# A hybrid decoder trunk on one core: attention's v by token rows for four heads at once, a gate's products in v's places, three low parts of a turn on GpSimd

## What is computed

```python
proj = jnp.einsum('bld,de->ble', x, w_in[l]) + b_in[l]
q_sb, k_sb, v_sb, u_ssm, q_mem, gate_logits = jnp.split(proj, splits, axis=-1)
sb = _stick_breaking_attention(q_sb, k_sb, v_sb)       # 8 heads of 128
p_sb = jnp.einsum('ble,ed->bld', sb, sb_w_out[l])
g = jax.nn.gelu(_s5(u_ssm, ...))
glu_a, glu_b = jnp.split(jnp.einsum('ble,ef->blf', g, ssm_w_glu[l]), 2, axis=-1)
p_ssm = jnp.einsum('ble,ed->bld', glu_a * jax.nn.sigmoid(glu_b), ssm_w_out[l])
p_mem = jnp.einsum('ble,ed->bld', _memory_attention(q_mem, mem, w_kv), mem_w_out[l])
gates = jax.nn.sigmoid(gate_logits).reshape(bsz, seq, 3, D_MODEL)
merged = gates[:, :, 0] * p_sb + gates[:, :, 1] * p_ssm + gates[:, :, 2] * p_mem
```

## Time and profile before

| | us |
|---|---|
| median of 3 runs | 2956.91 (2956.4 to 2957.02) |
| the profiled execution, its own time | 2957.04 |
| its span, first to last instruction | 2955.3 |
| PE busy in the span | 2935.8 |
| DVE busy | 1932.0 |
| ACT busy | 1371.5 |
| POOL busy | 46.6 |

### The profile page before, as it was taken

One profiled execution on the slowest core, in us unless ns is written; L12 is line 12 of the kernel. 1 busy time (PEld: TensorE's weight loads), 2 busy tenths in 40 slices (PEclk: granted clock), 3 DMA queues, 4 the chain that ended last, 5 costly groups with the idle time before them and its releaser, 6 DMA issues.

```text
span 2955.3 us, 37621 instructions
## 1 busy us (share of the span) xinstructions
PE 2935.8 (99%) x14068; PEld 2449.7 (83%) x14068; DVE 1932.0 (65%) x2754; ACT 1371.5 (46%) x1646; POOL 46.6 (2%) x117
## 2 busy tenths in 40 slices
PE   8999999999999999999999999999999999999999
PEld 7888888888888888888888888888888888888887
DVE  8899755555755555555699996555666555555556
ACT  6656544444544444444466554444444444444443
POOL 5000000000000000000000000000000000000000
PEclk9999999999999999999999999999999999999999
DMA  9666565656655555555556565665656555555554
GB/s 252 194 189 179 198 205 194 207 190 212 229 191 192 187 196 185 194 189 190 191 140 170 161 188 195 203 202 198 223 172 213 185 194 189 188 195 185 189 194 142
DMA packets 390020, 568.31 MB, mean 192 GB/s; under 512 B 20408, under 2 KB 194592, under 8 KB 389024
## 3 DMA queue, kind: packets, MB, share of 16 engines
q1 hardware_dynamic: 385712, 554.77, 58.5%
q10 hardware_dynamic: 4208, 12.21, 1.1%
HBM read 558.81 MB, written 8.13 MB: 192 GB/s over the span
## 4 chain that ended last, share of the span: by engine, by line
PE 97%; DVE 1%; ACT 1%; DMA 0%; issue 0%; SPq 0%; ACTq 0%; DVEq 0%
PE banks L1854 26%; PE banks L1856 26%; PE banks L1855 26%; PE banks L1829 9%; PE banks L1832 4%; PE banks L1844 1%; PE banks L2275 1%; PE banks L2209 1%; PE banks L2297 0%; DMA raw<-in_w_in 0%; DVE lo L1206 0%; PE banks L1846 0%; PE banks L2028 0%; PE banks L2040 0%; PE banks L2210 0%
## 5 line engine op out<-in xcount | busy, mean ns | idle before, releaser
L1206 DVE TENSOR_TENSOR lo<-raw,hi 128x1024 fp32r<-128x1024 f32 x1014 | 1232.0, 1225 | 957.5 <-ACT hi L736 870.6
L736 ACT ACTIVATE hi<-raw 128x1024 fp32r<-128x1024 f32 x932 | 977.8, 1059 | 1163.1 <-PE banks L1856 1155.1
L1854 PE MATMUL banks<-hi,xs 128*128 128x512 f32 x2176 | 852.0, 392 | 2.4 <-DVE xs L1349 2.4
L1856 PE MATMUL banks<-hi,xs 128*128 128x512 f32 x2176 | 847.3, 389 | 0.0
L1855 PE MATMUL banks<-lo,xs 128*128 128x512 f32 x2176 | 846.9, 389 | 0.0
L1854 PEld LDWEIGHTS banks<-hi,xs 128*128 128x128 f32 x2176 | 408.5, 188 | 86.6 <-DVE xs L1349 2.9
L1856 PEld LDWEIGHTS banks<-hi,xs 128*128 128x128 f32 x2176 | 408.4, 188 | 85.2
L1855 PEld LDWEIGHTS banks<-lo,xs 128*128 128x128 f32 x2176 | 408.7, 188 | 82.9
L1829 PE MATMUL banks<-xs,hi 128*128 128x512 f32 x960 | 307.1, 401 | 0.5 <-DVE lo L1206 0.5
L1854 PE MATMUL banks<-hi,hT 128*128 128x512 f32 x704 | 274.1, 389 | 0.0
L1856 PE MATMUL banks<-hi,hT 128*128 128x512 f32 x704 | 273.9, 389 | 0.0
(11 more groups left out here) (254 smaller groups left out, 2430.5 us busy)
## 6 DMA issues: line engine op xcount, KB each, us to landing
raw<-in_ffn_w_gate_up SPq DMA_DIRECT2D x176, 1024.0 KB, 5.0
raw<-in_w_in SPq DMA_DIRECT2D x156, 1024.0 KB, 5.2
raw<-in_ffn_w_down SPq DMA_DIRECT2D x88, 1024.0 KB, 4.9
raw<-in_w_o SPq DMA_DIRECT2D x32, 1024.0 KB, 5.0
raw<-in_sb_w_out SPq DMA_DIRECT2D x16, 1024.0 KB, 5.0
raw<-in_mem_w_kv SPq DMA_DIRECT2D x12, 1024.0 KB, 5.8
raw<-in_ssm_w_out SPq DMA_DIRECT2D x8, 1024.0 KB, 5.1
raw<-in_mem_w_out SPq DMA_DIRECT2D x8, 1024.0 KB, 5.1
```

Of the source, the lines that this page charges most:

```text
L736: act.activation(hi[:, hl_slot(ph, c, h), :], raw[:, slot, h * HALF:(h + 1) * HALF], ACT.Copy).then_inc(hi_ready, 1)
L1206: dve.tensor_tensor(lo[:, s, :], raw[:, slot, h * HALF:(h + 1) * HALF], hi[:, s, :].bitcast(F32), ALU.subtract).then_inc(lo_ready, 1)
L1854: pe.matmul(dst, xh, hi[:, s, w], start=first, stop=False)
L1856: return pe.matmul(dst, xl, hi[:, s, w], start=False, stop=last)
```

## The change

- v of heads 0 to 3 is computed in `group_half` form as four new chunks at the end of U, in banks 2 and 3; v of heads 4 to 7 in the old v places c = 2 and 5 of turns 0 and 1 (`wide`). DVE adds the bias and writes four heads at once (`v_rows`). The places c = 2 and 5 of turns 2 and 3 take gate 0. Transposes and copies of v go.
- The BL turn's own filler becomes gate 1 (`second_gate`, banks 0 and 1), and gate 1 leaves its place between the projections 0 and 1 in GLU. The number of chunks of a layer stays: U 8 (was 4), GLU 14 (was 18).
- Banks move: the state inputs to 5, 4, 6, 7; GLU's products to 4, 5, 6, 7, used twice (`GLU_BANK`).
- In BR turns other than the first of layer 0 the second half of chunks 3, 6 and 8 gets its low part from GpSimd (`POOL_AT`), five turns in all; DVE waits for it before it splits the next chunk.

```diff
-    "U": (1, [0, 1, 2, 3], [2] * 4),
+    "U": (1, [0, 1, 2, 3] * 2, [2] * 4 + [1] * 4),
-    "GLU": (1, ([2, 3, 0, 1] * 5)[:18], [1] * 4 + [4] * 2 + [1] * 12),
+    "GLU": (1, ([2, 3, 0, 1] * 4)[:14], [1] * 4 + [4] * 2 + [1] * 8),
-GLU_BANK = (0, 1, 4, 5, 6, 7, 0, 1)
+GLU_BANK = (4, 5, 6, 7, 4, 5, 6, 7)
+WIDE_AT = (2, 5)
+POOL_AT = (2, 5, 7)
...
+                for turn in range(1 - l, 3):
+                    for c in POOL_AT:
+                        gh = chunk_no("BR", l, turn, c + 1) * 2 + 1
+                        pool.wait_ge(hi_ready, gh + 1)
+                        pool.wait_ge(lo_ready, gh + HALF_CREDIT)
+                        pool.tensor_tensor(lo[:, hl_slot("BR", c + 1, 1), :],
+                                           raw[:, PHASES["BR"][1][c + 1], HALF:2 * HALF],
+                                           hi[:, hl_slot("BR", c + 1, 1), :].bitcast(F32), ALU.subtract
+                                           ).then_inc(lo_ready, 1)
...
+                        if shared and c - 1 in POOL_AT:
+                            dve.wait_ge(lo_ready, chunk_no(ph, l, i, c + 1) * 2 + HALF_CREDIT)
+                        if shared and c in POOL_AT:
+                            lo_half(PHASES[ph][1][c + 1], hl_slot(ph, c + 1, 0), 0, chunk_no(ph, l, i, c + 1) * 2)
+                        else:
+                            split_next(ph, l, i, c)
...
+                    def v_rows(g, dst, ready):
+                        dve.wait_ge(half_done, ready)
+                        dve.wait_ge(v_bias_in, 16 * (2 * l + g + 1))
+                        dve.tensor_tensor(dst[:].rearrange("p h m d -> p m h d"),
+                                          banks[:, 2:4, :].rearrange("p m (h d) -> p m h d", d=P),
+                                          v_bias[:].rearrange("p a (h d) -> p a h d", d=P)
+                                          .broadcast_to([P, TT, 4, P]), ALU.add).then_inc(v_ready, 1)
...
+                    pe.wait_ge(bu_copied, n * 4 + 3)
                     for t in range(TT):
                         ins = pe.matmul(S[:, t * T:(t + 1) * T], qm_f[:, t * P:(t + 1) * P], km_f[:], start=True,
                                         stop=True)
                     ins.then_inc(s_done, 1)
                     gemm(1, xs)
-                    gemm(2, xs)
+                    wide(2)
...
-                    got(2)
-                    v_turn(0, v_f, VO)
                     tri(0)
...
                         else:
-                            pe.wait_ge(tile_out, tile_no("GLU", l, 0, 1) + 1 + TILE_CREDIT)
+                            pe.wait_ge(tile_out, tile_no("GLU", l, 0, 2 * t - 3) + 1 + TILE_CREDIT)
...
                 branch_products("GLU", 0, GLU_SPANS, 0)
                 pe.wait_ge(tile_out, tile_no("GLU", l, 0, 7) + 1 + TILE_CREDIT)
-                gate_products("GLU", 0, GLU_SPANS, 1)
                 pe.wait_ge(merge_step, 20 * l + 1)
                 pe.wait_ge(glu_lo, 4 * l + 4)
                 branch_products("GLU", 0, GLU_SPANS, 1)
```

More of the change, by code:

```diff
@@ L454, in branch_turn @@
                                  (w, (t + (3 * SBW // P + 1)) * P), (w, (t + ((3 * SBW + SSMW) // P + 1)) * P)]
[L455 to L458, removed]
+                    for c, at in enumerate(cols):
+                        if at is None:
+                            load_block(ph, i, c, w, 4 * (2 * (t % 2) + WIDE_AT.index(c)),
+                                       2 * SBW + GROUP if t < 2 else GATE_COLS)
+                        else:
+                            load(ph, l, i, c, columns(*at))
+                    if t == 0:
+                        sp.wait_ge(v_ready, 2 * l + 1)
+                        load_v_bias(1)
                 if l == 0:
@@ L501, in _ @@
                 load_branch("GLU", 0, GLU_SPANS, 0, 0)
[L502 to L506, removed]
+                sp.wait_ge(attn_done, 12 * l + 15)
+                load_bias(0, 1)
                 load_branch("GLU", 0, GLU_SPANS, 0, 1)
-                sp.wait_ge(gate_in, 12 * l + 1)
-                load_bias(0, 2)
                 for c in range(4):
                     load_gate_block("GLU", 0, GLU_SPANS, 0, 2, c)
+                    if c == 2:
+                        sp.wait_ge(gate_in, 12 * l + 1)
+                        load_bias(0, 2)
                 load_branch("GLU", 0, GLU_SPANS, 0, 2)
@@ L907, in table @@
                     if q == 0:
[L908 removed]
+                        act.activation(tab[:].rearrange("p a c -> p (a c)"), bank[6][:, :], ACT.Copy).then_inc(tab_out, 1)
                         return
@@ L926, in tile @@
                             bias = bias_col(l, bias_tile)
-                        first_half(ph, l, i, c, bank[c % 2], done(ph, l, i, c), bias, scale)
-                        if l == 0 and turn == 1 and c % 2 and c < 8:
-                            save_mem(c // 2)
+                        k = TILE_AT[c]
+                        first_half(ph, l, i, k, bank[k % 2], done(ph, l, i, c), bias, scale)
+                        if l == 0 and turn == 1 and k % 2:
+                            save_mem(k // 2)
                     def copy_bu(j):
@@ L1027, in branch_turn @@
                     out_hi(0, VO, sbT[:, bass.ds(turn * 2, 1), 0:T])
-                    copy_v(1, S, vm_s, 2)
-                    tile(5, turn * 2 + 17)
+                    copy_vm()
                     softplus(1)
@@ L1103, in _ @@
                     glu_high(t)
-                for c in range(7, 18):
+                for c in range(7, 14):
                     split_next("GLU", l, 0, c)
-                    if c == 12:
+                    if c == 8:
                         gate_tanh(1, 4 * l)
-                    if c == 17:
+                    if c == 13:
                         gate_tanh(2, 4 * l)
@@ L1533, in branch_turn @@
                     split(0)
+                    if turn == 0:
+                        v_rows(0, v_first, chunk_no(ph, l, i, 0) * 2 + HALF_CREDIT)
                     if first:
@@ L1583, in branch_turn @@
                         split(6)
+                        if turn == 1:
+                            v_rows(1, v_last, chunk_no(ph, l, i, 6) * 2 + HALF_CREDIT)
                         scan_states(1, 5, 7)
@@ L1980, in _ @@
                     norm(l - 1, 1, first_state)
+                for c in range(4):
+                    for h in range(2):
+                        k = 4 * c + 2 * h
+                        group_half("U", l, 0, 4 + c, h, xs, k, 2, k == 0, k == KD - 2)
                 def table(q):
@@ L2006, in half, with wide @@
                     def half(c, x_t, h):
+                        k = TILE_AT[c]
                         if h == 0 and (turn or c):
-                            pe.wait_ge(tile_out, tile_no(ph, l, i, c) + 1)
-                        product(ph, l, i, c, h, bank[c % 2], x_t, 8 * h, h == 0, h == 1)
+                            pe.wait_ge(tile_out, tile_no(ph, l, i, k) + 1)
+                        product(ph, l, i, c, h, bank[k % 2], x_t, 8 * h, h == 0, h == 1)
+                    def wide(c):
+                        at = 2 * (turn % 2) + WIDE_AT.index(c)
+                        if at == 0:
+                            pe.wait_ge(v_ready, 2 * l + 1 + turn // 2)
+                        for h in range(2):
+                            k = 4 * at + 2 * h
+                            group_half(ph, l, i, c, h, xs, k, 2, k == 0, k == KD - 2)
                     def gemm(c, x_t):
```

224 lines of the change are left out of this document (115 added, 109 removed).

## The result

The changed kernel takes 2968.2 us (median of 6 runs, 2967.6 to 2969.26) against 2957.0 for the kernel before, a ratio of 1.0039 with a 95% interval of 1.0029 to 1.0049. The forecast was 2967.8. That closeness is partly luck: one cost in the sum was too high, one gain too small, and a cost that stood only among the rivals came true.

A forecast was written before the change was run, and what follows sets the result against it. The prediction took PE's streaming as the bound (busy 2935.8 of 2955.3 us). Its terms -5.7 + 8.0 + 7.5 + 1.5 - 0.5 = +10.8 on 2957.04 gave 2967.8 us, range 2957.5 to 2974.

The forecast's parts named there:

- wait of GLU's third group: GLU's third group of products waits for both takes of the first group: 0.75 us a layer, +1.5.
- rival 3: GLU: PE's 3.75 us wait lowers the granted clock, 1.7 us a fall, giving 2971; chance 0.12.
- Part 1: PE's streaming: v's transposes go (3.5 us less) and v's products take `group_half` form (2.2 less), -5.7.
- Part 2: Five shared turns: GpSimd's low parts hold DVE, PE waits 1.15 us a turn, `v_rows` adds 2.3 in two: +8.0.
- my stepping: Turn 1 chunk by chunk: PE waits 0.5 us at chunk 4, 0.3 at chunk 7, 0.35 at chunk 9.
- Part 3: GLU: PE waits 3.75 us a layer for `merge(0)`, +7.5, and 0.75 before the third group, +1.5.
- Part 4: The start: `b_blk` in time (1.0 us), `vm_s` stays, new waits of 0.75 and 0.9; sum about -0.5, bounds -3 and +2.
- The wait for `copy_bu`: The start: the scores `S` wait for the first `copy_bu` because the bank is now shared, 0.75 us.
- the one for U's third v chunk: The start: its late load makes the low part ready at 55.3 where PE wants it at 54.4, 0.9 us.
- what was taken to stay: The start: the 1.4 us PE idles for `vm_s`, said to stay as ACT's run and PE shorten alike.
- Rival 1: Shared turns: GpSimd's halves run beside DVE's scan, part 2 becomes 0, giving 2959.8 us; chance 0.17.
- rival 2: GLU: the wait for `merge(0)` is mostly covered, 1.3 us instead of 3.75, giving 2962.9; chance 0.05.

The follow-up runs named there:

- experiment 1: Changed kernel with POOL_AT empty, so DVE forms all low parts of the branch turns again: 2962.8 us.
- experiment 6: Kernel before with nothing changed but three low parts on GpSimd in five turns: 2960.3 us, ratio 1.0012.
- experiment 8: Changed kernel with GLU's banks moved against bank waits and POOL_AT = (7,), one low part of a turn on GpSimd: 2950.2 us.
- experiment 7: Changed kernel with POOL_AT empty and GLU's banks moved, plus useless two-input and one-input GpSimd work in layer 0: 2966.0 us in one run.
- experiment 2: Changed kernel with GLU's merge(0) one place earlier on DVE, between the two low parts of chunk 9: 2960.5 us.

## Why the prediction came out right

Term by term, in us over both layers:

| term | predicted | shown |
|---|---|---|
| products and transposes PE no longer streams | -5.7 | -5.4 |
| GpSimd's low parts, with `v_rows` | +8.0 | +6.3 |
| wait for `merge(0)` | +7.5 | +7.5 |
| wait of GLU's third group | +1.5 | +1.6 |
| start, turn 0 | -0.5 | -2.0 |
| clock behind the merge wait | rival 3, 3.4 | +3.4 |
| sum | +10.8 | +11.4, measured +11.2 |

**Part 1** held: a turn without waits went from 65.77 to 65.09, 0.68 for the predicted 0.72, times eight. The transposes take 0.22 a head in the rows, as read. The rest, 0.24 for two chunks, says that matmuls of 256 columns are dearer than their columns. The Trainium skill's figure (TensorE: Matmul & The Clock Gate, section Back-to-back issue gap), by which the two forms would differ by 0.02 us a chunk, would have given 0.48 a turn; the turns don't agree with it.

**Part 2** was right in place and mechanism, and 1.7 too high. Set beside experiment 1, whose turns have no waits, PE falls back in turn 2 of layer 0 at chunk 4 by 0.35, at chunk 7 by 0.16 and at chunk 9 by 0.25 + 0.07, and nowhere else. I had 0.5, 0.3 and 0.35. In turn 1 it is 0.43, 0.16, then 0.44 at chunk 8 and 1.02 at chunk 9, 2.05 for my 2.3. Two sizes were off. The first is the time for which a GpSimd half holds DVE beyond what it saves: 2.14 to 2.2 held, against my 2.25, with 1.14 saved. Set against experiment 1, DVE in turn 1 stands 1.02 later behind the first half and 2.07 behind the second, then makes up 0.5 before chunk 7's low parts, and stands 2.63 later behind the third: 1.02 to 1.05 a half, not 1.1. The 0.5 is the second: my stepping had 0.19 for the idle time used up there. The rest lies in leads known to a tenth or so. One reading behind the 2.25 was loose: the 1.2 that DVE lost at 47 us is little more than one operation of 448 columns (1.05), not one and a half. Experiments 1, 6 and 8 show the mechanism with and without its parts; experiment 7 shows that DVE's two-input operations are held and its PSUM ones are not, and that a one-input operation on GpSimd holds only in its first 0.9 us. The Trainium skill (SBUF — State Buffer, section SBUF: two separate sides) has GpSimd and DVE lock their shared ports for a whole instruction. For two-input work on GpSimd the rows agree, with DVE's scan steps at 2.73 instead of 0.59, and with its PSUM operations at 1.21. For one-input work they don't: the lock is over after 0.9 of 2.77 us.

**Part 3** held to 0.05: 3.74 for the merge and 0.8 for the third group. Both could be read off the rows of before, since each engine's order is fixed: the merge's place behind the low parts of chunk 9, the copy by ACT that they need, and the durations. What I missed is that a wait has a price behind its end. I had put that at 0.12 as rival 3 and had its size (1.7 a fall) right, from the earlier trace rows; it happened in both layers. The rows that I set against it, a wait of 1.4 that kept the clock, were no evidence for one of 3.75, and the text said as much before it gave the small chance. The Trainium skill (TensorE: Matmul & The Clock Gate, section HAM oscillation) warned of it, and the trace agrees: 0.66 and 0.72 behind these waits. It deserved more weight than the absence of a row.

**Part 4** missed most for its size: -2.0, not -0.5, within its bound of -3. Turn 0 went from 71.01 (first `state_inputs` matmul to that of turn 1) to 68.28, of which 0.7 is part 1. Who PE waited for, in the kernel before (43 to 120 us) and in the changed kernel (64 to 140 us):

```profile
PE banks L2133 <- ACT vm_s L956: 1.4, 1, 1.4
PE banks L1992 <- ACT b_blk L831: 1.0, 1, 1.0
PE banks L1992 <- ACT stage L913: 0.8, 2, 0.5
PE banks L1829 <- DVE lo L1206: 0.5, 1, 0.5
```

```profile
PE banks L2190 <- ACT vm_s L987: 0.9, 1, 0.9
PE banks L2158 <- ACT scan L965: 0.8, 1, 0.8
PE banks L2039 <- ACT stage L943: 0.3, 1, 0.3
```

The wait for `copy_bu` came as foreseen (0.8) and `b_blk` went as foreseen (1.0). Two steps failed. The first is the one for U's third v chunk: I added 0.9 for its late load, and PE waited for no low part there. The second is what was taken to stay: the waits for `vm_s`, `stage` and a low part each became 0.5 shorter. Together that is 1.7 less waiting; the other 0.3 is PE's own busy time in the turn. The sum was wrong in itself, too: the terms that it names, -1.0, +0.75 and +0.9, make +0.65 and not -0.5, and nothing is said of where the other 1.15 should come from. No run of mine took the start apart, so why `vm_s` came earlier stays open. What lies ahead of turn 0 isn't counted here: PE got there 21.2 later than in the kernel before, 0.6 less than four v chunks of 5.44, and the old kernel itself got there at 49.65 in one profile and at 48.99 in another (experiment 6, which is the same up to there).

Rival 1 (GpSimd beside DVE for nothing) is refuted by experiment 1, rival 2 (the merge covered) by the wait of 3.74 and by experiment 2. The range's lower end should have been 2957.3 by its own terms, not 2957.5; nothing hangs on it. What is left of the total: the errors of -1.7 and -1.5 and the clock's +3.4 nearly cancel. The sum was right to 0.4 us, its terms only to 1 or 3; with the mechanism of rival 3 in it, as it happened, it would have said 2971.2.

## What to carry to other kernels

Count a helper engine's instruction at the time for which it holds its neighbour, not at the time that it saves: a low part of 2.4 us on GpSimd took 1.14 off DVE and held it for 2.2, because the next thing in DVE's order read two SBUF operands. Where filler work is taken from between two users of the same banks, look at what the second one waits for and whether other banks are free; here two other bank numbers gave back 10.9 us, and with the third group's banks and without GpSimd's low parts the loss of 11.2 us became a gain of 7.1. Price a long TensorE wait with what follows it: 3.7 us of waiting cost 5.4.

## What the runs showed of the hardware

- GpSimd and DVE, both with two SBUF inputs of 1024 columns: DVE's operation takes 2.99 on average instead of 1.22, GpSimd's 3.09 instead of 2.40. DVE's operations with one input in PSUM stay at 1.21.
- GpSimd with one SBUF input of 1024 columns (2.77 us): a two-input operation of DVE is held only if it starts in the first 0.9 us of GpSimd's, by up to 0.9; later it runs in its 1.23.
- The granted clock kept 1.00 behind the wait of 1.5 us in GLU and fell to its half level at each wait of 3.7 (six in the three profiles that have them), once before the wait had ended, for about 3 us in the changed kernel; the same wait cost 2.7 us in layer 0 of experiment 1, so the price of a fall isn't fixed.
- A fall can also come behind two waits of only 0.8 and 1.1 us (22 us, experiment 8), at a place where other profiles with the same waits keep 1.00.
